# 235 places at which an engine no longer waits for its own last operation

## The reference, cut to what matters

```python
def reference(x, ...):
    x = first_block(x, ...)    # RWKV-7 time mixing (16 heads) and differential attention (8 heads), gates, MLP
    x = second_block(x, ...)   # gated delta rule, gated linear attention, HGRN; branches; grouped mixture of experts
    return third_block(x, ...) # forgetting, block-sparse, stick-breaking and windowed attention
```

```python
def step(S, inp):
    rt, wt, kt, vt, at, bt = inp
    sa = jnp.einsum('bhvk,bhk->bhv', S, at)
    S = S * wt[:, :, None, :] + sa[..., None] * bt[:, :, None, :] + vt[..., None] * kt[:, :, None, :]
    y = jnp.einsum('bhvk,bhk->bhv', S, rt)
    return S, y
...
w = -jax.nn.softplus(-(w0 + jnp.tanh(wd) @ w2)) - 0.5
decay = jnp.exp(-jnp.exp(w))
a = jax.nn.sigmoid(a0 + ad @ a2)
```

## Time and profile before

| | |
|---|---|
| time, median of 3 runs | 3372.89 us (3369.41 to 3378.97) |
| profiled execution | span 3363.8 us from the first to the last instruction; its own device time is not given, the median of the runs lies 9.1 us above the span |
| PE busy | 3044.7 us, 91% |
| PEld busy | 2466.5 us, 73% |
| DVE busy | 1632.5 us, 49%, 2885 instructions |
| ACT busy | 1218.2 us, 36%, 2081 instructions |
| POOL busy | 831.8 us, 25%, 808 instructions |
| granted TensorE clock | mean 0.928 of full speed |
| DMA | 259.79 MB, mean 77 GB/s |

### The profile page before, as it was taken

The page is one execution under the profiler, slowest core; times in us unless marked ns, Lnnn a source line. Parts: engine busy times, 40 slices in busy tenths (PEclk is TensorE's granted clock), DMA queues, the critical chain, the costliest instruction groups (busy, mean ns, idle before and its releaser), DMA issues. The chain is left out here.

```text
span 3363.8 us, 58589 instructions
## 1 busy us (share of the span) xinstructions
PE 3044.7 (91%) x24118; PEld 2466.5 (73%) x24118; DVE 1632.5 (49%) x2885; ACT 1218.2 (36%) x2081; POOL 831.8 (25%) x808
## 2 busy tenths in 40 slices
PE   7789898989889999999889889888889999889898
PEld 6777787778767778886667677767679998556566
DVE  3555655455524343342454465566565656542432
ACT  2333333434322243232434343534254444342342
POOL 4222222211122100001445365550000002423242
PEclk9889898989789999999899889989999999778899
DMA  3111111111023323332212122214225556311112
GB/s 127 33 33 39 30 37 33 39 30 36 27 96 119 119 82 94 94 94 60 60 49 72 48 70 70 69 51 160 83 88 172 169 163 183 118 35 51 35 54 66
DMA packets 94811, 259.79 MB, mean 77 GB/s; under 512 B 10672, under 2 KB 10672, under 8 KB 93264
## 3 DMA queue, kind: packets, MB, share of 16 engines
q1 hardware_dynamic: 81968, 209.11, 20.7%
q0 software_dynamic: 7680, 35.40, 3.1%
q10 hardware_dynamic: 4896, 11.54, 0.9%
HBM read 236.08 MB, written 19.92 MB: 76 GB/s over the span
## 5 line engine op out<-in xcount | busy, mean ns | idle before, releaser
L452 PE MATMUL psum<-arena,ring 128*128 128x512 f32 (+3 forms) x6792 | 1631.5, 359 | 14.9 <-DVE arena L384 8.4
L452 PEld LDWEIGHTS psum<-arena,ring 128*128 128x128 f32 (+1 forms) x6792 | 1153.0, 194 | 211.7 <-issue 35.2
L452 PE MATMUL psum<-arena 32*32 32x32 f32 (+12 forms) x12500 | 900.2, 255 | 221.8 <-DVE arena L384 64.8
L452 PE MATMUL psum<-arena,arena 128*128 128x512 f32 (+3 forms) x3872 | 985.3, 350 | 33.6 <-DVE arena L384 11.6
L452 PEld LDWEIGHTS psum<-arena 32*32 32x32 f32 (+9 forms) x12500 | 631.9, 142 | 437.9 <-issue 149.8
L452 PEld LDWEIGHTS psum<-arena,arena 128*128 128x128 f32 (+2 forms) x3872 | 658.2, 188 | 156.1 <-issue 31.9
L377 ACT ACTIVATE arena<-psum 128x512 f32<-128x512 f32 (+15 forms) x660 | 301.5, 457 | 768.8 <-PE psum L452 594.6
L396 POOL CAST ring<-ring 128x512 fp32r<-128x512 f32 x332 | 221.0, 666 | 1289.2 <-DMA ring<-in_w 1281.4
L384 DVE TENSOR_TENSOR arena<-arena 128x528 f32<-128x528 f32 (+9 forms) x638 | 360.1, 564 | 224.9 <-ACT arena L369 135.2
L384 DVE TENSOR_TENSOR ring<-ring,arena 128x1024 fp32r<-128x1024 f32 (+1 forms) x250 | 293.5, 1174 | 338.6 <-ACT arena L377 336.0
L384 POOL TENSOR_TENSOR ring<-ring,ring 128x512 fp32r<-128x512 f32 x332 | 445.6, 1342 | 26.7
(11 more groups left out here) (51 smaller groups left out, 970.2 us busy)
## 6 DMA issues: line engine op xcount, KB each, us to landing
ring<-in_w SPq DMA_DIRECT2D x202, 512.0 KB, 3.5
ring<-in_w SPq DMA_DIRECT2D x356, 256.0 KB, 2.6
bg<-arena ACTq DMA_DIRECT2D x24, 256.0 KB, 2.2
yd<-arena ACTq DMA_DIRECT2D x10, 512.0 KB, 5.2
arena<-bg POOLq DMA_DIRECT2D x1, 3072.0 KB, 16.6
arena<-in_x SPq DMA_DIRECT2D x1, 2112.0 KB, 14.8
od<-arena POOLq DMA_DIRECT2D x8, 256.0 KB, 2.4
oy<-arena POOLq DMA_DIRECT2D x8, 256.0 KB, 3.0
```

What stands on the lines that cost most here:

```text
L452: self.last_ins = self.eng.matmul(out, l, r, start=start, stop=stop, skip_group_check=skip)
```

## The change

`own` no longer waits. It notes what it owes, and `ready` (before the next operation) or `wait_ge` (before a wait for another engine) pays it by `settle`, unless the place is marked `apart()`. At 235 places of the three programs the operation and the waits in front of it are so marked. Operations and their order stay as they were on every engine, but for ScalarE's function tables: a table of names now loads them explicitly, and one load fewer is made, between the hyperbolic tangent and the first sigmoid.

```diff
@@ Engine
     def wait_ge(self, sem, n):
         if self.seen.get(sem.num, 0) < n:
+            self.settle()
             self.seen[sem.num] = n
             self.eng.wait_ge(sem, n)
@@ own
         ins.then_inc(*self.book.up(sem, event))
-        self.last = (sem, self.book.count[sem])
-        self.wait_ge(self.book.sem(sem), self.book.count[sem])
+        self.last = self.owed = (sem, self.book.count[sem])
+
+    def settle(self):
+
+        if self.owed and not self.alone:
+            sem, n = self.owed
+            self.owed = None
+            self.wait_ge(self.book.sem(sem), n)
+
+    def apart(self):
+
+        self.alone = True
+        return self
+
+    def ready(self):
+
+        self.settle()
+        self.alone = False
+        return self.eng
@@ Scalar, and each operation of Vector in the same way
     def copy(self, out, a, *event, scale=1.0):
-        self.own(self.eng.activation(out, a, ACT.Copy, scale=scale), event)
+        self.own(self.ready().activation(out, a, ACT.Copy, scale=scale), event)
@@ act_rwkv, prep
-        A.wait_ge(*at("rw_w", hp))
-        A.act(h2(m.e), out_of(K, 2, T, "rw_e", hp), ACT.Sigmoid, "rw_e", hp, bias=p["w0"][:, hp:hp + 1])
...
-        A.wait_ge(*at("rw_cum", hp))
-        A.act(m.pm, m.pm, ACT.Exp, "rw_pm", hp, scale=-EH)
-        A.act(m.e, m.cum, ACT.Exp, scale=EH)
+        A.apart().wait_ge(*at("rw_w", hp))
+        A.apart().act(h2(m.e), out_of(K, 2, T, "rw_e", hp), ACT.Sigmoid, "rw_e", hp, bias=p["w0"][:, hp:hp + 1])
...
+        A.apart().wait_ge(*at("rw_cum", hp))
+        A.apart().act(m.pm, m.pm, ACT.Exp, "rw_pm", hp, scale=-EH)
+        A.apart().act(m.e, m.cum, ACT.Exp, scale=EH)
         A.act(m.cum, m.cum, ACT.Exp, "rw_exp", hp, scale=-EH)
@@ dve_diff
-        V.wait_ge(*at("df_exp", hd, i, 0))
-        V.rec(sc[0][:, 2:3], sc[0][:, 1:2])
-        V.wait_ge(*at("df_exp", hd, i, 1))
-        V.rec(sc[1][:, 2:3], sc[1][:, 1:2])
+        V.apart().wait_ge(*at("df_exp", hd, i, 0))
+        V.apart().rec(sc[0][:, 2:3], sc[0][:, 1:2])
+        V.apart().wait_ge(*at("df_exp", hd, i, 1))
+        V.apart().rec(sc[1][:, 2:3], sc[1][:, 1:2])
         V.tt(sc[1][:, 2:3], sc[1][:, 2:3], lam[0:qw, 4:5], MUL)
```

More of the change, by code:

```diff
@@ L356, with tables @@
 LEAD = 9
+TABLES = {ACT.Exp: "natural_log_exp_and_others", ACT.Ln: "natural_log_exp_and_others", ACT.Sigmoid: "sigmoid_and_others",
+          ACT.Tanh: "sigmoid_and_others", ACT.Silu: "silu_and_others", ACT.Sqrt: "sqrt_and_others"}
 class Scalar(Engine):
-    logs = False
-    def act(self, out, a, f, *event, bias=0.0, scale=1.0, accum=None):
[L364 to L369, removed]
+    table = None
+    def tables(self, f):
+        name = TABLES.get(f)
+        if name and name != self.table:
+            self.eng.preload_act_table_set(name)
+            self.table = name
+    def act(self, out, a, f, *event, bias=0.0, scale=1.0, accum=None):
+        self.tables(f)
+        self.own(self.ready().activation(out, a, f, bias=bias, scale=scale, accum_out=accum), event)
@@ L730, in act_root @@
     A, n = K.A, 2 if T > 512 else 1
-    A.wait_ge(*K.book.at("sum", name))
-    A.inv_root(h2(rs) if n == 2 else rs, out_of(K, n, T, "root", name), "root", name, scale=scale, bias=eps)
+    A.apart().wait_ge(*K.book.at("sum", name))
+    A.apart().inv_root(h2(rs) if n == 2 else rs, out_of(K, n, T, "root", name), "root", name, scale=scale, bias=eps)
 def dve_rms(K, name, x, wcol, out, T, rs, o0=0):
@@ L1954, in dve_mlp @@
                 dve_hidden(K, m, half, k - 1)
-            V.wait_ge(*at("slab", "mlp", i))
+            V.apart().wait_ge(*at("slab", "mlp", i))
             if half or k > 1:
-                V.wait_ge(*(at("H_sq", half, k - 2) if k > 1 else at("H_sq", 0, 14 + k)))
-            V.stt(m.rl[k % 2], out_of(K, 1, T, "relu", half, k), 0.0, m.rs2, MAX, MUL, "relu", half, k)
+                V.apart().wait_ge(*(at("H_sq", half, k - 2) if k > 1 else at("H_sq", 0, 14 + k)))
+            V.apart().stt(m.rl[k % 2], out_of(K, 1, T, "relu", half, k), 0.0, m.rs2, MAX, MUL, "relu", half, k)
             i += 1
@@ L1966, in dve_mlp @@
                 i += 1
-            V.wait_ge(*at("slab", "mlp", i - 1))
-            V.tt(xs, xs, out_of(K, 1, T, "h3", half, k), ADD, "h3", half, k)
+            V.apart().wait_ge(*at("slab", "mlp", i - 1))
+            V.apart().tt(xs, xs, out_of(K, 1, T, "h3", half, k), ADD, "h3", half, k)
     V.stage_end("dve", "block1")
@@ L3318, in dve_group @@
     left = R["tmp"][:, 20:24]
-    V.ms(left, 1.0)
+    V.apart().ms(left, 1.0)
     for g in range(4):
@@ L3336, in dve_slots @@
         V.tt(here, here, before, ADD)
-        V.tt(all_, all_, before, ADD)
+        V.apart().tt(all_, all_, before, ADD)
     over, f = R["tmp"][:, 32:48], R["f"][:, 0:16]
@@ L3888, in qk_tile @@
             yield
-        V.wait_ge(*at("fx_proj", t, n))
-        V.stt(x, bk("fx_" + n, t), 0.125 if n == "q" and not gain else 1.0, m.rs, MUL, MUL, "fx_" + n, t)
+        V.apart().wait_ge(*at("fx_proj", t, n))
+        V.apart().stt(x, bk("fx_" + n, t), 0.125 if n == "q" and not gain else 1.0, m.rs, MUL, MUL, "fx_" + n, t)
         if gain:
             yield
-            V.wait_ge(*at("fx_root", t, n))
+            V.apart().wait_ge(*at("fx_root", t, n))
             gq = m.gain[KIND[t]] if n == "q" else p[KIND[t] + "g"][:, 1:2]
-            V.stt(x, x, gq, s1, MUL, MUL, "fx_qk", t, n)
+            V.apart().stt(x, x, gq, s1, MUL, MUL, "fx_qk", t, n)
     def v_tile(t):
@@ L4131, in _ @@
             for i, (k, v) in enumerate(small):
-                K.V.ms(K.c[k], v, *(("eps",) if i == len(small) - 1 else ()))
+                K.V.apart().ms(K.c[k], v, *(("eps",) if i == len(small) - 1 else ()))
             K.V.wait_ge(*book.at("con"))
```

844 lines of the change are left out of this document (422 added, 422 removed).

## The result

The changed kernel takes 3323.73 us (median of 4 runs, 3312.64 to 3330.16) against 3373.44 us (4 runs, 3369.41 to 3378.97): ratio 0.9847, 95% interval 0.9824 to 0.987, 49.7 us faster. The forecast was 3319 us.

The account below looks back on a forecast made before the run. TensorE's work and its waits on ScalarE/VectorE chains (319 us idle) were taken to bound the kernel. 15.7 us in pairs plus 27.2 elsewhere made 42.9; with 11 from the clock, 54 us, so 3372.9 became 3319 us, range 3268 to 3360.

Parts of the forecast that it names:

- Hand-offs, 0.06 us: Where an operation waits for another engine and its own, dropping the own wait, with one left, saves 0.06 us.
- ScalarE back to back, 0.13 us: Consecutive ScalarE operations: a start without the own wait saves 0.13 us each; lower bound 0.03 us.
- VectorE back to back, 0.06 us: Consecutive VectorE operations: a start without the own wait saves 0.06 us, taken between bounds of 0 and 0.13 us.
- 1.96 us a pair: Decays, softmax and copies in one pair of heads: 1.96 of 10.9 us idle time saved; 15.7 us over eight pairs.
- Elsewhere, 14% of 194 us: Remaining idle time in heads, mixers and third block: a sampled attention's 14% share applied to 194 us, saving 27.2 us.
- The sum, 42.9 us of idle time: TensorE idle time saved over the whole kernel, 42.9 of 319 us: 15.7 us in pairs plus 27.2 us elsewhere.
- The clock, 11 us more: TensorE's mean clock rises by 0.0096 as idle time shrinks, priced at 22 us over the span; half taken, 11 us.
- Table load, copies and other work beside TensorE, 0: ScalarE and VectorE savings while TensorE computes, including the removed 1.28 us table load, are worth nothing: queued matmuls cover them.
- VectorE gives nothing: Rival: VectorE's next operation starts where it did, with or without the wait; 5.8 us missing, 3325 us; chance 0.25.
- nothing arrives: Rival: TensorE's waits have second reasons behind the first, or dropped waits never held an operation; 3370 us; chance 0.06.
- The strong clock: Rival: shorter waits in pairs of heads double the clock's gain from 22 to 44 us; about 3280 us; chance 0.17.
- The slower case: Rival: denser work shifts slow stretches, above all in pairs of heads, mean clock falling over 0.024; about 3385 us; chance 0.03.

Follow-up runs that it names:

- VectorE alone: Change applied to VectorE and GpSimd only, ScalarE waiting as before but with the change's table loading, against the kernel before: 3334.80 us, 0.9892.
- The run with the order turned: Kernel before with all own waits kept, the two waits of a hand-off swapped, and the change's table loading: 3365.36 us, 0.9981 of before.
- the three fills: The change plus ten, three and two constant matmuls in TensorE's three longest waits of each pair of heads: 3279.93 us, 0.9713 of before.
- the turned runs: Two waits swapped: in the kernel before, 3365.36 us; in the change, at all places keeping two waits 3319.14 us, only at chosen hand-offs 3310.30 us.
- the second trace of the change: Profile of the unaltered change run once more on another chip, against the kernel before: 3325.10 us, 0.9859.
- The same ten matmuls: Ten constant matmuls filling TensorE's longest wait of each pair: in the kernel before 3370.05 us, 0.9991; in the change 3301.10 us, 0.9784 of before.

## Why the prediction was right, by its steps

- *Hand-offs, 0.06 us*: right. 0.09 to 0.03 in the chain of the earlier trace rows; PE's wait there fell by 0.20 for 0.18 forecast.
- *ScalarE back to back, 0.13 us*: right. 0.14 in the exponentials, 0.126 by medians. The decays' wait fell by 0.64 us, to the forecast's hundredth, which is partly luck: the two starts among the copies gave 0.16 us each (1.20 to 0.88), not 0.13.
- *VectorE back to back, 0.06 us*: too small; 0.106 in the masked products, 0.114 by medians. The row it was nearest to was the wrong guide: the gap with the wait is 0.03 us on both engines, and without it both overlap. The bound of 0.13 was nearly the value.
- *The Trainium skill* (VectorE: DVE Perf Modes, section "The DRAIN you can't avoid": chaining without semaphores is no faster) is contradicted by these runs: 0.106 us a start in the masked products, and 37 us for VectorE alone. The same page's section "Two Vector instructions with no wait between them" treats an instruction that is not held as free to start before the earlier ones end, and that is what these traces show.
- *1.96 us a pair*: 3.13 measured (10.92 to 7.79). The masked products gave 0.35 us for 0.24, the waits around the softmax and masks 1.12 for 0.73 (both VectorE's price), the copies 0.35 as forecast; 0.67 lies in waits that the sum did not list. So the pair's sum was too small by 1.2 us, 9 us in eight pairs.
- *Elsewhere, 14% of 194 us*: 52.3 less the eight pairs' 25.0 and the large products' 2.5 leaves 24.8 us for 27.2 forecast. The total fits, but partly by luck, since one share for all places did not hold: the heads outside the pairs gave nothing (24.7 us in the whole stage) for 6.3, the mixers 10.5 us of 88.5 (12%), the third block 14.7 of 60.2 (24%). *Large products, 0*: 1.7 + 0.8 us.
- *The sum, 42.9 us of idle time*: 52.3 measured. The mis-sized terms are VectorE's start and the pair's sum that it feeds.
- *The clock, 11 us more*: this step failed. Its price was right: over the 44 runs of before a mean clock higher by 0.001 goes with 2.2 us less, as in the forecast's 22 us for 0.0096. But the clock did not follow: the median is 0.926 over those runs and 0.926 over the nine runs of the change. The first profiled execution has 0.925, down from 0.928, the second 0.928. In the six pairs the time at the low clock grew from 109 to 123 us in the first and 130 in the second; 14 us more at half speed are about 7 us lost. The clock did not follow idle time in proportion. In the first trace it fell in whole stretches of 10.2 us, two to a pair, next to the waits that were left: from 396.5 us, where the wait of 3.24 us ends at 397.31, and from 451.1, where that of 1.13 us ends at 450.76.
- *The time*: 9 us too little idle time and 11 us too much clock cancel, so that 3319 us came within 5 us of 3323.7. That closeness is luck; the steps on the waits are what held.
- *Table load, copies and other work beside TensorE, 0*: not contradicted, and not tested alone. The run with the order turned has the table load gone and every own wait in place, and is only 6 us faster than its runs of before.
- *Rivals*: "VectorE gives nothing" forecast 3325 us, nearer to the measured 3323.7 than 3319 is, so the time could not tell the two apart. The run with VectorE alone (37 us) refutes it, and the result refutes "nothing arrives". The strong clock did not come with the change, but the three fills on top of it did bring one of that size: 3323.7 - 3279.9 = 44 us. The slower case, denser work with more time at the low clock, came in the pairs of heads but not over the kernel: 503 us at the low clock in the first trace and 478 in the second, against 487 before, and no mean clock lower by 0.024.

## What to carry over

In chains that cross engines, a wait for the engine's own last operation costs in two ways: about 0.12 us back to back, on both engines, and 0.06 us at a hand-off where it makes a second wait. It can go only where the operation does not read what the unfinished one writes; the change keeps it there. Where two waits are needed, the one that is met last belongs on the operation itself. And once waits have become short, look at TensorE's clock before counting on more: filling three of the waits that remain in a pair was worth 44 us, nearly as much as the change.

## What the runs showed of the hardware that I had not expected

- A start without a wait overlaps the one ahead by 0.093 us on ScalarE and 0.080 us on VectorE. The Trainium skill (ScalarE: Activation LUTs, section "What ACT_TABLE_LOAD costs") gives an overlap of about 93 ns for back-to-back activations; the trace agrees.
- The separate wait instruction costs 0.06 us only when its wait is met last; met early it costs nothing (hand-offs of 0.03 us with two waits in the turned runs, but for ScalarE's from TensorE, 0.086 us).
- Six pairs of heads of the change took the same 109.2 us, each with 20.5 us at the low clock, though before they differed by 4 us. What keeps them in step was not tried; in the second trace of the change the six took 658.1 us instead of 655.4.
- The same ten matmuls were worth nothing clear of noise in one kernel (0.9979 to 1.0003) and 21 us or more in the other.
